# A gated-delta mixer placed round by round, its output projection split by inputs, and an expert choice issued whole

## The reference

```python
def peer_ffn(h, wq, subkeys, u, v):
    q = (xt @ wq).reshape(T, PEER_HEADS, 2, PEER_HALF)
    s = jnp.einsum('thpc,hpnc->thpn', q, subkeys)
    s_top, i_top = lax.top_k(s, PEER_TOPK)                      # 16 of 128, twice
    cand = s_top[:, :, 0, :, None] + s_top[:, :, 1, None, :]    # 256 candidates
    best, pos = lax.top_k(cand.reshape(T, PEER_HEADS, 256), PEER_TOPK)
    ...
    act = jax.nn.gelu(jnp.einsum('cd,ced->ce', xb, u[eb]), approximate=False) * gb
    return jnp.einsum('ce,ced->cd', act, v[eb])
```

```python
def even_mixer(h, w_in, conv_a_w, dn_conv_w, a_log, dt_bias, dn_norm_w, w_out):
    p = h @ w_in
    a_gate_in, a_gate_out, a_h, qkv, z, beta_raw, alpha_raw = jnp.split(p, splits, -1)
    y_a = a_gate_out * causal_dwconv(a_gate_in * a_h, conv_a_w)
    qkv = jax.nn.silu(causal_dwconv(qkv, dn_conv_w))
    q, k = l2_norm(q) * DN_HEAD_DIM ** -0.5, l2_norm(k)
    beta = jax.nn.sigmoid(beta_raw)
    g = -jnp.exp(a_log) * jax.nn.softplus(alpha_raw + dt_bias)
    o = gated_delta_rule(q, k, v, beta, g)      # chunks: a triangular solve each, then a recurrence
    o = rms_norm_2(o, dn_norm_w) * jax.nn.silu(z)
    return jnp.concatenate([y_a, y_b], -1) @ w_out
```

## Time and profile before

| | |
|---|---|
| median of 3 runs | 1885.73 us (1884.34 to 1886.17) |
| profiled execution | 1890.34 us, its span 1888.5 us |
| granted clock of PE, mean | 0.938 |
| PE busy | 1632.0 us (86%), 9325 matmuls |
| DVE busy | 1209.6 us (64%) |
| ACT busy | 835.8 us (44%) |
| POOL busy | 377.1 us (20%) |
| gathers (queue 0) | 36864 packets, 268.45 MB, 34.5% of the 16 DMA engines' span |
| chain that ended last | PE 59%, DMA 17%, DVE 13%, ACT 8% |

### The profile page before, as it was taken

The page is one execution under the profiler, slowest core; times in us unless marked ns, Lnnn a source line. Parts: engine busy times, 40 slices in busy tenths (PEclk is TensorE's granted clock), DMA queues, the critical chain, the costliest instruction groups (busy, mean ns, idle before and its releaser), DMA issues.

```text
span 1888.5 us, 24071 instructions
## 1 busy us (share of the span) xinstructions
PE 1632.0 (86%) x9325; PEld 1229.6 (65%) x9325; DVE 1209.6 (64%) x2395; ACT 835.8 (44%) x1706; POOL 377.1 (20%) x327
## 2 busy tenths in 40 slices
PE   7688898588977788878887987879999999999999
PEld 6678798545533333322242766869999976579999
DVE  5666465687877778545654657536776546657764
ACT  5635454344444434333443643225554434445542
POOL 1200011344534444433442002102000200010000
PEclk9889899899988888999999988989999999899999
DMA  6313242599999999999999221113444521025544
GB/s 248 112 69 111 91 177 90 214 373 426 425 421 399 390 387 380 415 427 427 427 427 401 81 76 45 47 61 140 178 179 152 187 109 45 23 74 189 185 160 153
DMA packets 63593, 421.15 MB, mean 223 GB/s; under 512 B 8180, under 2 KB 11512, under 8 KB 15608
## 3 DMA queue, kind: packets, MB, share of 16 engines
q0 software_dynamic: 36864, 268.45, 34.5%
q1 hardware_dynamic: 23952, 148.70, 21.8%
q10 hardware_dynamic: 2664, 2.47, 0.4%
HBM read 418.54 MB, written 1.05 MB: 222 GB/s over the span
## 4 chain that ended last, share of the span: by engine, by line
PE 59%; DMA 17%; DVE 13%; ACT 8%; issue 2%; POOL 0%; SPq 0%; DVEq 0%; ACTq 0%
PE bank L303 57%; DMA uv<-in_uv,idx 16%; DVE lows L366 3%; ACT L315 2%; DVE uv L1312 2%; PE bank L308 1%; PE bank L2406 1%; ACT dg L315 1%; DVE cacc L319 1%; ACT wp L311 1%; ACT acts L315 1%; DMA slabs<-in_w_in 1%; POOL uv L1427 0%; ACT wf L311 0%; DVE t L319 0%
## 5 line engine op out<-in xcount | busy, mean ns | idle before, releaser
L303 PE MATMUL bank<-uv,dg 128*128 128x512 f32 x1024 | 501.9, 636 | 119.2 <-ACT dg L315 117.7
L303 PEld LDWEIGHTS bank<-uv,dg 128*128 128x128 f32 x1024 | 195.0, 200 | 415.7 <-ACT dg L315 212.1
L1312 DVE CUSTOM_DVE_ANT_0 uv<-uv,htok 128x1024 f32<-128x1024 f32 x256 | 313.0, 1223 | 187.6 <-DMA uv<-in_uv,idx 185.8
L1427 POOL DMA_INDIRECT uv<-in_uv,idx x256 | 292.7, 1143 | 393.2 <-PE bank L303 329.7
L366 DVE TENSOR_TENSOR lows<-slabs,wp 128x2048 fp32r<-128x2048 f32 (+1 forms) x78 | 168.3, 2158 | 54.6 <-ACT wp L311 54.6
L303 PE MATMUL bank<-hn,lows 128*128 128x272 f32 (+2 forms) x704 | 200.9, 285 | 0.0
L481 POOL TENSOR_TENSOR sqT<-sqT 128x256 f32<-128x256 f32 (+1 forms) x42 | 54.5, 1298 | 712.4 <-ACT sqT L315 709.7
L311 ACT ACTIVATE wp<-slabs 128x2048 fp32r<-128x2048 f32 (+1 forms) x78 | 140.5, 1802 | 78.1 <-DMA slabs<-in_dn 27.9
L366 DVE TENSOR_TENSOR lows<-slabs,whl 128x2048 fp32r<-128x2048 f32 (+1 forms) x52 | 110.4, 2124 | 49.4 <-ACT whl L311 49.3
L315 ACT ACTIVATE acts<-acts 128x1 f32<-128x1 f32 x256 | 50.3, 197 | 199.3 <-DVE acts L1312 198.9
L303 PE MATMUL bank<-hh,lows 128*128 128x272 f32 x448 | 134.8, 301 | 0.0
(11 more groups left out here) (365 smaller groups left out, 3050.3 us busy)
## 6 DMA issues: line engine op xcount, KB each, us to landing
slabs<-in_up SPq DMA_DIRECT2D x44, 1024.0 KB, 4.8
slabs<-in_w_in SPq DMA_DIRECT2D x28, 1024.0 KB, 4.8
slabs<-in_dn SPq DMA_DIRECT2D x32, 704.0 KB, 4.0
slabs<-in_wkv SPq DMA_DIRECT2D x8, 1024.0 KB, 4.8
slabs<-in_w_out SPq DMA_DIRECT2D x8, 1024.0 KB, 4.8
slabs<-in_pq SPq DMA_DIRECT2D x8, 1024.0 KB, 4.8
slabs<-in_wq SPq DMA_DIRECT2D x4, 1024.0 KB, 4.9
slabs<-in_wo SPq DMA_DIRECT2D x4, 1024.0 KB, 4.8
```

The source lines that it names most:

```text
L303: ins = T.e.matmul(pr[2] if len(pr) > 2 else out, pr[0], pr[1], start=(start and k == 0), stop=(stop and k == len(pairs) - 1), skip_group_ ...
L1312: V.e.tensor_tensor_reduce(u_, u_, htok[:, n, :], 1.0, 0.0, ALU.mult, ALU.add, acts[:, n, e_:e_ + 1]).then_inc(*V.up("dot", q))
L1427: G.e.indirect_dma_start(uv[q % NU][:, :], None, d["uv"][:, :], bass.IndirectOffsetOnAxis(ap=idx[:, n, e_:e_ + 1], axis=0)).then_inc(s_uv[ ...
```

## The change

1. *Expert choice.* `peer_plan` issues the first head's choice whole before the scores of head 1, with `tokens` behind its seventh step; before, the two were woven. The load of `sub` moves from the start of `peer_scalar` to `xat_scalar`, behind mixer 1.
2. *Order of w_in2.* The value slabs 6 and 7 come ahead of z slab 5. The gates' matmuls move behind piece (2,1), and their ACT and DVE work behind the eighth convolution.
3. *Plan.* `mixer2_plan` places by round number: pieces, `decay`, its columns (`dcols`), `xs`, and each slab's split in two parts, ACT's ("high") in a round and DVE's ("low") in the next.
4. *w_out2 by inputs.* Four slabs of 4 input tiles x 512 outputs, 16 quarter pieces of 12 matmuls (4 tiles x 3 terms); each result is added into the residual. Those on input tiles 0 to 3 stand in rounds 66 to 73, in the recurrence, with their parts in rounds 62 and 63; those on tiles 4 to 7 stay behind the list.
5. `rsf` moves to a tile of its own (`sqT[:, 3]`).

```diff
-          ("w_in2", 14, 8, 256), ("w_out2", 4, 8, 256), ...
+          ("w_in2", 14, 8, 256), ("w_out2", 4, 4, 512), ...
+MIXED2 = [0, 1, 2, 3, 4, 6, 7, 5] + list(range(8, 14))
...
         def peer_plan():
-            out = scores_of(0) + [("tokens",)]
-            out += [x for x in woven([[x] for x in choice_of(0, 0)], scores_of(1), 2)]
+            first, second = scores_of(0), choice_of(0, 0)
+            out = first + second[:7] + [("tokens",)] + second[7:] + scores_of(1)
...
-        SIDE2 = [("pj", "w_in2", 4 + i, j) for i in range(10) for j in range(2)]
-        MIX2 = SIDE2[:4] + woven(delta_rounds(20), SIDE2[4:], 5)
+        def mixer2_plan():
+            turns = delta_rounds()
+            side = [[] for _ in turns]
+            pieces = [("pj", "w_in2", i, j) for i in MIXED2[4:] for j in range(2)][1:]
+            pieces += [("pj", "w_out2", i, j) for i in range(2) for j in range(4)]
+            side[1].append(("decay", 0, 0))
+            side[3].append(("dcols", 0, 0))
+            out = [pieces.pop(0)]
+            for n, x in zip((1, 3, 5, 7, 12, 16, 21, 24, ..., 61, 66, 67, 68, 69, 70, 71, 72, 73), pieces):
+                side[n].append(x)
+            for p, n in zip(range(7, 18), (4, 8, 13, 27, 34, 41, 49, 53, 57, 60, 74)):
+                side[n].append(("high", p, 0))
+                side[n + 1].append(("low", p, 0))
+            for c in range(NC):
+                side[30 + 2 * c].append(("xs", c, 0))
+            for c in range(4):
+                side[62 + c // 2].append(("part", c, 0))
...
-        rsf = cva[:, 0, 0:T1]
+        rsf = sqT[:, 3, 0:T1]
...
+        def out2_tensor(i, j):
+            n, o, was = PLACE["w_out2", i], pbank("w_out2", i, j)[:, 0:T2], PBANK["w_out2", i, j][1]
+            w = weights(n)
+            split_tensor(n)
+            T.wait_ge(*V.at("ev", *was))
+            for q in range(4):
+                c = 4 * (i // 2) + q
+                T.wait_ge(*V.at("m2lo", c))
+                ins = mm(o, [(w[p][:, q, j * P:(j + 1) * P], HH[r][:, c, :]) for p, r in TERMS], q == 0, q == 3)
...
+        def out2_vector(i, j):
+            c = 4 * (i % 2) + j
+            V.wait_ge(*T.at("pj", "w_out2", i, j))
+            V.e.tensor_tensor(xT[:, c, :], pbank("w_out2", i, j)[:, 0:T2], xT[:, c, :], ALU.add)...
...
         def side2_vector(i, j):
-            if j == 0:
-                ahead(N_L2 + i, split_vector)
...
         def mix2_scalar():
             ...
+            ahead(N_L2 + 4, split_scalar)
+            side2_scalar(4, 0)
+            silu2_scalar(7)
             A.wait_ge(*V.at("be_raw"))
             act(be, be, ACT.Sigmoid).then_inc(*A.up("beta"))
```

More of the change, by code:

```diff
@@ L1135, in xat_scalar @@
             stage_wait(A, "mix1")
+            A.e.dma_start(sub[:, :, :], d["subT"][:, :, :]).then_inc(s_sub, 16)
             for i in range(4):
@@ L1999, in mix2_vector, with decay_vector @@
             stt(gg, tmp2, -1.0, tmp2, ALU.mult, ALU.max).then_inc(*V.up("dabs"))
-            pre2_vector(1, 0)
-            conv2_vector(1)
-            pre2_vector(1, 1)
-            ahead(N_L2 + 1, split_vector)
-            conv2_vector(2)
+            side2_vector(4, 0)
+            conv2_vector(7)
+            ahead(N_L2 + 4, split_vector)
+            for x in MIX2:
+                if x[0] == "pj" and x[1] == "w_in2":
+                    side2_vector(x[2], x[3])
+                elif x[0] == "pj":
+                    out2_vector(x[2], x[3])
+                elif x[0] == "high":
+                    pass
+                elif x[0] == "low":
+                    split_vector(N_L2 + x[1])
+                elif x[0] == "part":
+                    part2_vector(x[1])
+                elif x[0] == "decay":
+                    decay_vector()
+                elif x[0] == "dcols":
+                    V.wait_ge(*T.at("dcols"))
+                    for ci, (s, ln) in enumerate(CHUNKS):
+                        V.e.tensor_copy(cols[0:ln, ci, 0, :], B[3][0:ln, 4 * ci:4 * ci + 4]).then_inc(*V.up("dcols", ci))
+                    V.wait_ge(*V.now())
+                elif x[0] == "chunk":
+                    chunk_vector(x[1], x[2])
+                elif x[0] == "rec":
+                    rec_vector(x[1], x[2])
+                elif x[0] == "xs":
+                    final_norm_vector(x[1])
+                else:
+                    delta_vector(*x)
+            for c in range(4, NC):
+                part2_vector(c)
+            for i in (2, 3):
+                ahead(PLACE["w_out2", i], split_vector)
+                for j in range(4):
+                    out2_vector(i, j)
+                    c = 4 * (i - 2) + j
+                    if c:
+                        gain_vector("fn0", xT, "fn0", T2, FF[0][0], c - 1)
+            gain_vector("fn0", xT, "fn0", T2, FF[0][0], NC - 1)
+        def decay_vector():
             V.wait_ge(*A.at("dln"))
@@ L2073, in mix2_scalar @@
             act(ea4, vcol("alog", 0, 4), ACT.Exp).then_inc(*A.up("alog"))
-            for i in range(1, 4):
-                ahead(N_L2 + i, split_scalar)
-                for j in range(2):
-                    tap2_scalar(i, j)
-                    silu2_scalar(2 * i + j - 1)
-            silu2_scalar(7)
             for x in MIX2:
-                if x[0] == "pj":
+                if x[0] == "pj" and x[1] == "w_in2":
                     side2_scalar(x[2], x[3])
+                elif x[0] in ("pj", "low", "xs", "decay", "dcols"):
+                    pass
+                elif x[0] == "high":
+                    split_scalar(N_L2 + x[1])
+                elif x[0] == "part":
+                    part2_scalar(x[1])
                 elif x[0] == "chunk":
```

123 lines of the change are left out of this document (57 added, 66 removed), and 2 rows, old and new, of the table STREAM.

## The result

The changed kernel takes 1894.02 us (median of 5 runs, 1891.87 to 1896.61), the kernel before 1885.87 (5 runs, 1884.34 to 1887.46): ratio 1.0044, interval 1.003 to 1.0059. It is 8 us slower; forecast were 11 us faster. The profiled execution took 1891.87 us, its span 1890.1. Executions of one program differ here: 23 of before in a later session lie between 1882.5 and 1891.6 us, within 5 of their median, and 12 of one experiment (e10) between 1876.4 and 1895.8, up to 14 from it. The profile of before that the prediction read took 1890.34 us, over all five timed runs of before. So stages are compared over several profiles, and kernels by ratios of timed runs.

A forecast was written before the change was run, and what follows sets the result against it. DMA engines bound the expert lookup, PE mixer 2 and the feed forward. The expert choice's -6.0 and mixer 2's -5 gave -11 us: 1879.3 profiled, 1874.7 us as timed; range 1862 to 1888.

The forecast's parts named there:

- Part 1: Expert choice ahead of the lookup: first head's choice made whole starts the gathers earlier; -6.0 us, bounds -6.9 and -4.5.
- (a): Mixer 2 to the end of the first slabs: gate matmuls move behind slab 2, a 1.50 us wait goes; -2.2 us.
- (b): Mixer 2 up to the chunks' start: late gates with five table loads, and further PE waits; +3.6 us here.
- the walk: Mixer 2's new order followed on all engines with the durations of before; -11.1 us at full clock.
- (c): Chunk start-up in mixer 2: POOL's kbe now stalls DVE's AT steps instead of a split; +2.4 us in all so far.
- (d): Levels in mixer 2: 7 pieces instead of 6, one every 4 rounds, 60.0 us after 62.45; -2.4 us.
- (e): Recursion, output and output projection: half of w_out fills the recursion's waits, 64.6 us after 75.7; -11.1 us.
- (f): Mixer 2's slow clock behind PE's idle spells: +6 us added, bounds 0 and 14.
- C: Rival, chance 0.1: slow pieces lengthen steps ACT and DVE wait for, mixer +12 to +15 us; 1893 us.
- D: Rival, chance 0.08: DMA rate limits the whole expert lookup, so the earlier gathers' 6 us are lost; 1880.7 us.

The follow-up runs named there:

- e10: Changed kernel with the output projection by outputs again, 8 whole pieces behind the list: ratio 1.0018 to the kernel before.
- e2: Kernel before with only the first head's choice made whole and the load of sub moved: ratio 0.9973 to the kernel before.
- e3: Changed kernel with the first choice and the load of sub put back, mixer 2's changes alone: ratio 1.0077 to the kernel before.
- e12: Changed kernel with unread matmuls in PE's five long waits ahead of the chunks: ratio 0.9977 to the kernel before.
- e13: e12 with unread matmuls in five more PE waits, from the chunks to the output projection: ratio 0.9917 to the kernel before.
- e15: e10 with unread matmuls in PE's long waits, front and back: ratio 0.9898 to the kernel before.
- e5: Changed kernel with the gates' work on PE, DVE and ACT back behind the first convolution: ratio 1.0012 to the kernel before.
- e8: Changed kernel with the gates' sigmoid, exponentials and logarithm replaced by the loaded silu, four table loads fewer, results wrong: ratio 1.0008 to the kernel before.

## Why the prediction was wrong

- **Part 1, -6.0: right.** Measured -5.1 (e2) and -5 to -6 (e3). Its chain is 7.0 us shorter from the sub-keys' product to the first gather (6.7 in the sum).
- **(a) and (b) at full clock: right.** First sum at 54.8 us of the mixer (54.0 in the walk), idle 12.04 (11.7), kk at 102.15 in e12 (102.1).
- **(c) and (d): right at full clock.** First 16x16 transpose 120.0 in e12 (121), recursion 181.0 (181). The stall of (c) moved as it was said to: beside POOL's product kbe four AT steps of DVE take 3.23 us in the changed kernel, and 1.12 behind it.

```profile
1147.57 2.48 POOL L2177 TENSOR_TENSOR kbe<-kbt,ebT 128x1088 f32<-128x1088 f32 x1 [130.59 <-DVE kbt L1713]
1147.75 3.23 DVE L321 SCALAR_TENSOR_TENSOR AT<-bbt,cols,con 128x128 f32<-128x128 f32 x4
...
1150.98 1.12 DVE L321 SCALAR_TENSOR_TENSOR AT<-bbt,cols,con 128x128 f32<-128x128 f32 x4
```

- **(e), -11.1: wrong by 4.6 at full clock.** From the recursion to the feed forward the walk had 64.6 us; e13 has 69.2. Both hold 1.7 us of low clock (in e13 by its clock records), though the sum is called one at full clock. The by-outputs kernel e15 has 65.0: the step took the quarters as filling idle time and had no cost for their place ahead of the output norm's broadcasts (argued above, not tried alone).
- **(f), the clock, +6: the step that failed.** The walk at full clock gives a mixer of 256.5 - 11.1 = 245.4 us; measured are 264.2. Of the 18.8 between, 14.0 go when PE is kept busy (264.2 to 250.2; from the second profile's 267.2 it would be 17), where 6 were charged and 14 was the upper bound, and 4.6 are (e). I had worked out 26 us of slow clock for before and then charged the new order 6, as if fewer long waits meant less. By the same account the changed kernel pays 214.4 - 189.6 = 25 us, as much as before. The account is somewhat high: by the clock records of the profiles the slow clock adds 22.0 and 20.0 us to PE's busy time in mixer 2 of before, and 21.5 and 24.9 in the changed kernel. Waits of 2.5 to 3 us bring slow pieces too, and it has eleven waits over 1.5 us where before has nine. Idle time grew by 8.7, slow time stayed: that is the +7.7 of the two profiles.
- **Rivals.** C was right in place and time (1893 us, slow pieces between the first sum and kk, measured 1894.0), and I gave it 0.1; its size is partly luck, as it had the mixer at +12 to +15 where +7.7 (9.8 in the means) was measured. "A slow stretch with PE busy lasts about 5 us at most" was no argument against it: there were four short ones in a row. Its point of decision, kk at 113, was too late, since (e) held less to eat. D is out (e2, e3).
- **Against expectations in the waits.** The 12 us wait looks worst; taking away its half in two ways (e5, e8) gave 5 us at kk, while keeping PE busy in all five, without shortening the first, gave 8 there (110.0 to 102.2).

Open: why the clock falls for longer behind mixer 2 in some executions of the same code than in others, and what the quarters cost by their place alone. And the parts of a split apart were tried in the changed kernel alone.
